# Expert rows fetched and turned one place at a time, 13 weight slots, and the smallest expert last

## What is computed

```python
def moe_ffn(h, comb, wg, wu, wd):
    out = jnp.zeros_like(h)
    for e in range(N_EXPERTS):
        ye = (jax.nn.silu(h @ wg[e]) * (h @ wu[e])) @ wd[e]
        out = out + comb[:, e:e + 1].astype(h.dtype) * ye
    return out

    h2 = (rms_norm(x, p['norm2_w']) * (1 + sc2) + sh2).reshape(bt * s, D_MODEL)
    comb = route(h2, w_router, router_bias)      # two weights a token, the rest zero
    y_moe = moe_ffn(h2, comb, ...).reshape(bt, s, D_MODEL)
    x = x + g2 * y_moe
    y = rms_norm(x, final_norm_w)
```

## Time and profile before

| | us |
|---|---|
| median of three runs (lowest, highest) | 1006.31 (1005.38, 1008.71) |
| the profiled execution: its own time | 1004.06 |
| its span, first to last instruction | 1002.3 |
| busy in the span: PE, DVE, ACT, POOL | 944.0, 441.4, 233.2, 145.3 |
| mean rate of the DMA engines over the span | 236 GB/s |
| mean granted PE clock (share of full speed) | 0.986 |

### The profile page before, as it was taken

How to read it: one execution, slowest core, us unless ns; L and a number is a source line. 1 busy time by engine, 2 the same in 40 slices (tenths; PEclk the granted TensorE clock), 3 DMA queues, 4 the chain that set the end, 5 groups by cost and what they waited for, 6 DMA issues and landing times.

```text
span 1002.3 us, 18836 instructions
## 1 busy us (share of the span) xinstructions
PE 944.0 (94%) x7702; PEld 659.7 (66%) x7702; DVE 441.4 (44%) x1094; ACT 233.2 (23%) x461; POOL 145.3 (14%) x236
## 2 busy tenths in 40 slices
PE   5999999999999999999999999999899988797895
PEld 2667666666666666666666777767599856564671
DVE  3221234676346986656641531134643342322316
ACT  2231222243263322232252300002231110110013
POOL 0000232343020343322300000011200000000010
PEclk9999999999999999999999999999999999899997
DMA  9943344564455655665443533342579999999973
GB/s 376 392 165 126 127 169 143 197 225 162 161 193 197 255 196 179 227 218 202 159 172 126 224 122 127 126 168 98 214 291 387 419 419 420 417 420 420 421 281 118
DMA packets 46541, 236.98 MB, mean 236 GB/s; under 512 B 6672, under 2 KB 10352, under 8 KB 23152
## 3 DMA queue, kind: packets, MB, share of 16 engines
q1 hardware_dynamic: 44480, 229.83, 59.7%
q0 software_dynamic: 1520, 5.34, 1.6%
q10 hardware_dynamic: 448, 0.50, 0.1%
HBM read 212.34 MB, written 23.31 MB: 235 GB/s over the span
## 4 chain that ended last, share of the span: by engine, by line
PE 73%; DMA 15%; DVE 6%; issue 2%; ACT 2%; SPq 1%; POOL 0%; POOLq 0%; DVEq 0%
PE pjB L884 15%; PE pjA L884 15%; DMA ring<-in_w 8%; PE pjA L1282 7%; PE pjB L1282 7%; DMA bp<-in_w 4%; PE states L1456 4%; PE states L1468 3%; PE states L1459 2%; DMA yd<-hF 2%; PE states L893 1%; PE bank L1019 1%; PE states L1261 1%; PE states L1019 1%; PE bank L1248 1%
## 5 line engine op out<-in xcount | busy, mean ns | idle before, releaser
L884 PE MATMUL pjA<-hF,ring 128*128 128x320 f32 x608 | 171.9, 436 | 0.5 <-ACT regA L1719 0.5
L884 PE MATMUL pjB<-hF,ring 128*128 128x320 f32 x608 | 171.8, 435 | 0.0
L884 PEld LDWEIGHTS pjA<-hF,ring 128*128 128x128 f32 x608 | 113.2, 190 | 50.7 <-issue 7.0
L884 PEld LDWEIGHTS pjB<-hF,ring 128*128 128x128 f32 x608 | 113.3, 190 | 48.6 <-issue 4.7
L1456 PE MATMUL states<-ring,oF 128*32 128x128 f32 x720 | 80.5, 273 | 2.1 <-DMA ring<-in_w 1.7
L1456 PEld LDWEIGHTS states<-ring,oF 128*32 128x32 f32 x720 | 78.0, 110 | 5.5 <-issue 2.7
L1459 PE MATMUL states<-ring,oF 128*32 128x384 f32 x720 | 80.7, 491 | 0.0
L2764 DVE TENSOR_TENSOR oF<-oF,states 128x256 f32<-128x256 f32 (+1 forms) x15 | 7.2, 483 | 139.9 <-PE states L1468 70.4
L2470 DVE TENSOR_TENSOR G<-G 128x320 f32<-128x320 f32 x32 | 47.1, 1510 | 0.0
L2076 POOL TENSOR_TENSOR G<-regA,G 128x128 f32<-128x128 f32 (+1 forms) x32 | 19.0, 594 | 192.3 <-ACT G L1775 192.3
L2173 POOL DMA_DIRECT2D yd<-hF x1 | 0.6, 640 | 244.2 <-DVE hF L2755 244.2
(11 more groups left out here) (565 smaller groups left out, 1518.2 us busy)
## 6 DMA issues: line engine op xcount, KB each, us to landing
ring<-in_w SPq DMA_DIRECT2D x144, 1024.0 KB, 8.5
rF<-in_w SPq DMA_DIRECT2D x11, 1024.0 KB, 18.6
bcF<-in_w SPq DMA_DIRECT2D x11, 1024.0 KB, 20.6
bp<-in_w SPq DMA_DIRECT2D x10, 1024.0 KB, 19.0
G<-in_ss SPq DMA_DIRECT2D x16, 512.0 KB, 4.7
out_ss_new<-G SPq DMA_DIRECT2D x16, 512.0 KB, 2.9
G<-csd SPq DMA_DIRECT2D x16, 320.0 KB, 3.5
G<-in_sg SPq DMA_DIRECT2D x4, 1024.0 KB, 6.4
```

What stands on the lines that cost most here:

```text
L884: mm = pe.matmul(pj[g % 2][:, 0:T], w[:, k, half * P:half * P + P], hF[:, k, :], start=(k == 0), stop=(k == KT - 1))
```

## The change

The places: `FULL_AT` becomes (0, 1, 4, 6, 8, 10), six instead of eight. Only places 0 and 1 are fixed; the smallest expert stands in place 15, with two blocks. The loop is written out, without a hardware loop.

The slots: 13 instead of 9. The new ones lie in `xsF` (two, loaded before the experts start) and in `regA` (two, loaded right behind the branch: the first when x has been turned, the second when the token rows are no longer needed).

The rows: `xd` is read place by place, 96 or 64 rows (`rows_in`, SP), turned by PE (`turn_rows`) and copied by ACT and DVE (`copy_rows`) into one of two buffers. The later turnings of weights and gates (`turn_late` 6 to 11) go behind the `gate_up` of places 6 to 11. A store of 96 rows of x behind `xd`'s end, early in the kernel, makes reading at full width defined.

The stores to `yd` are issued by ACT instead of SP.

The end: place 15's tokens are finished in a layout of their own, 64 rows as two halves of 512 values. PE collects in one bank, for these rows, what the other expert, the gate and x have given (`base_rows`, three tiles); DVE multiplies the last `down` with the weight and the gate (`weighted_half`), adds the bank, and scales. The three output tiles are written without these rows' last part, and then POOL writes the finished rows over them by an indirect DMA, which waits for all three. The additions of x for the first two tiles move from DVE to POOL.

```diff
-SLOTS = R + 3
+SLOTS = R + 7
+KNOWN = R + 5
-FULL_AT = (0, 1, 2, 5, 8, 11, 14, 15)
-FIXED_AT = (0, 1, E - 1)
+FULL_AT = (0, 1, 4, 6, 8, 10)
+FIXED_AT = (0, 1)
...
+            def rows_in(p):
+                at = sp.value_load(meta[0:1, ROW_AT + p:ROW_AT + p + 1], min_val=0, max_val=XROWS)
+                sp.wait_ge(s_xt2, max(p - 2, 0))
+                sp.dma_start(rowsB[p % 2][0:cap_of(p), :], d["xd"][bass.ds(at, cap_of(p)), :]).then_inc(s_xe[p % 2], 16)
...
             with sp.If(few(sp)):
+                sp.wait_ge(s_tm, 6)
+                sp.dma_start(slot(KNOWN), d["w"][chunk_row(*SEQ[KNOWN])]).then_inc(slot_ready(KNOWN)[0], 16)
                 sp.wait_ge(s_xd, 16 * 6)
-                sp.dma_start(xs01[:, 0, :], d["xd"][0:P, :]).then_inc(s_xe[0], 16)
-                sp.dma_start(xs01[:, 1, :], d["xd"][P:2 * P, :]).then_inc(s_xe[1], 16)
-                sp.wait_ge(s_oss, GH + 1)
-                sp.dma_start(hT, d["xd"][2 * P:XROWS, :].rearrange("(a p) c -> p a c", p=P)).then_inc(s_xe[1], 16)
...
+                rows_in(1)
+                sp.wait_ge(s_oss, GH + 2)
+                sp.dma_start(slot(KNOWN + 1), d["w"][weight_row(2) + SEQ[KNOWN + 1][1]]).then_inc(slot_ready(KNOWN + 1)[0], 16)
+                rows_in(2)
+                refill(0, 0, 4)
+                rows_in(3)
...
+                for p in range(3, LAST):
+                    refill(p, 0, 4)
+                    if p + 3 < E:
+                        rows_in(p + 3)
+                    refill(p - 1, 4, 6)
...
+                gate_up(0)
+                turn_rows(1)
+                gate_up(1)
+                turn_rows(2)
+                down(0)
+                turn_rows(3)
+                down(1)
+                gate_up(2)
+                for p in range(3, LAST):
+                    gate_up(p)
+                    turn_rows(p + 1)
+                    if TM_EARLY <= p < 12:
+                        turn_late(p)
+                    if p == 12:
+                        last_rows()
+                    down(p - 1)
+                down(LAST - 1)
+                gate_up(LAST)
+                turn_act()
+                base_rows(0)
+                down(LAST)
+                base_rows(1)
+                base_rows(2).then_inc(s_gw, 1)
+                row_sums()
...
+            def base_rows(t):
+                pe.wait_ge(s_base if t == 2 else s_x3, 1 if t == 2 else t + 1)
+                for h in range(2):
+                    mm = each_row(b[4], selL, hT[0:TT[t][2], t, 512 * h:512 * h + 512], t, h, t == 0, t == 2)
+                return mm
...
+                for t in range(2):
+                    pool.wait_ge(s_gm, t + 1)
+                    pool.tensor_tensor(hT[:, t, :], hT[:, t, :], xT[:, t, :], ALU.add).then_inc(s_x3, 1)
+                pool.wait_ge(s_tix, 2)
+                pool.wait_ge(s_f, 4)
+                pool.wait_ge(s_out, 16 * 4)
+                pool.indirect_dma_start(out=d["yrows"], out_offset=bass.IndirectOffsetOnAxis(ap=tix[:, 0:1], axis=0),
+                                        in_=zF_, in_offset=None).then_inc(s_last, 16)
...
+                summed(0).then_inc(s_gm, 1)
+                gated_up(LAST)
+                turned_last()
+                summed(1).then_inc(s_gm, 1)
+                cm(summed(2))
+                cm.wait()
+                dve.tensor_tensor(hT[0:NSAMP, 2, :], hT[0:NSAMP, 2, :], xT[0:NSAMP, 2, :], ALU.add).then_inc(s_base, 1)
+                final(0, 0, y2)
+                dve.wait_ge(s_gwc, 3)
+                weighted_half(0)
+                weighted_half(1)
+                final(1, 1, y2)
+                dve.wait_ge(s_zl, 2)
+                dve.wait_ge(s_gw, 2)
+                dve.tensor_tensor(zL, zL, b[4][:, :], ALU.add).then_inc(s_zl, 2)
+                final(2, 2, y2)
```

## The result

The changed kernel takes 1020.45 us (median of 4 runs, 1019.66 to 1023.96) against 1007.08 for the kernel before in the same job: ratio 1.014, 95% interval 1.011 to 1.017. It is slower by 1.4%. 997.4 had been forecast, a range of 987 to 1005.5, and a chance of 0.07 for slower. The profiled execution's span is 1018.3 us against 1002.3, and against 993.4 in the forecast.

A forecast was written before the change was run, and what follows sets the result against it. It took the weight stream's end and the tail behind it as the bounds: stream end 961, first gathered rows 965.9, plus 17.5 and 10.0 gives a span of 993.4 (1002.3 before), time 997.4, range 987 to 1005.5 us.

The forecast's parts named there:

- The stream: Weight stream after the branch: fewer bytes, earlier start and less idle time move its end from 971.0 to 961 us.
- rival 4: Row loads in SP's single queue starve the weight stream, DMA idling at every place: slower; 0.07 together with anything unforeseen.
- a DMA share under 0.95: Sign set beforehand: such a share between 750 and 940 us would show the forecast wrong.
- Start and idle time: Weight stream: loads into new slots start at 716.5, winning 0.9 us; closing the stall at 730 to 750 wins 6.1.
- Six large places for eight at nothing: Experts: fewer three-block places save PE 11.3 us, costed at nothing because loads hide them from place 5 on.
- The store of place 14: Stream's end: issued on ACT's queue at 948.9, it takes 7.8 us and lands at 956.7, 14.3 us earlier.
- the prediction's first reading: Engines take turns between queues with work, so place 14's store on ACT's queue overtakes the weight chunks, taking 7.8 us.
- the second: Issuing engines save only issue time, so place 14's store takes 16.1 us and the end comes 8.3 us later.
- rival 3: Place 14's store is no quicker on ACT's queue (16.1 us); tail shifts 8.3 us, time 1005.7, no change; chance 0.08.
- The tail: After the stores: first gathered rows at G = 965.9, PE's work until G + 17.5, then 10.0 us to 993.4.
- The end part: Behind PE's last base rows: DVE's addition and scaling, output, final scatter and waits, 10.0 us in all.
- One sign: Sign set beforehand: more than 31 us from the first gather issue to the end would show the forecast wrong.

The follow-up runs named there:

- e1_wide: Changed kernel, row loads bringing the same bytes as pieces of 2 or 3 KB into all 128 partitions (wrong rows): 995.67 us, ratio 0.988.
- e1_from_w: Changed kernel, row loads reading from the weights' tensor instead of xd, into the same partitions (wrong rows): 1023.99 us.
- e1_one_row: Changed kernel, row loads from place 3 on bringing one row, same issue point and wait (left-over rows used): 988.98 us.
- e1_halves: Changed kernel, result kept, rows loaded as halves (some as quarters) over all 128 partitions, PE turning 128x128 blocks: 995.24 us, ratio 0.988.
- e2_mid: Changed kernel, row loads from place 3 on written 32 partitions higher (32 to 95, or 32 to 127), same 4 KB pieces: 1004.28 us.
- e3_upper: Changed kernel, row loads from place 3 on written to the uppermost partitions (64 to 127, or 32 to 127): 1024.17 us.
- e3_pair: Changed kernel, each row load from place 3 on split into two DMAs, half to partitions from 0, half to partitions from 64: 1019.25 us.
- e2_rows128: Changed kernel, result kept, every row load bringing 128 rows into all partitions whatever the place's size: 1003.07 us, ratio 0.996.
- e2_sp_store: Kernel of e1_halves, stores to yd issued by SP behind the refills instead of by ACT: 1000.11 us, ratio 0.994.
- e2_eight: Kernel of e1_halves with eight places of three blocks instead of six: 996.6 us, ratio 0.990.
- e3_tail_dve: Kernel of e1_halves, the tail's two additions of the base rows on DVE instead of POOL: 994.17 us, ratio 0.987.

## Why the prediction was wrong, step by step

All kernels' numbers together, in us but for the rate (GB/s, 750 to 950; time: median, or the one run):

```
kernel        time     span     excess  rate
before        1007.08  1002.3    8.7    416
changed       1020.45  1018.3   32.1    377
e1_wide        995.67   995.1    7.5    420
e1_from_w     1023.99  1022.2   35.6    371
e1_one_row     988.98   987.0    8.9    420
e1_halves      995.24   993.1    7.1    420
e2_mid        1004.28  1002.2   15.8    407
e3_upper      1024.17  1022.2   33.7    372
e3_pair       1019.25  1017.5   29.0    382
e2_rows128    1003.07   998.1    6.7    420
e2_sp_store   1000.11   998.8    7.2    420
e2_eight       996.60   996.4    7.1    420
e3_tail_dve    994.17   992.3    7.0    420
```

The kernel before, measured beside each group of these runs, took 1006.96 to 1007.08, so the groups can be compared. From the first gather to the end of the span the changed kernel takes 34.8 us and its variants 34.0 to 35.4 (e1_one_row 36.8): nearly all that sets them apart lies ahead of the tail.

**The step that failed** is in "The stream": "the rows are read expert by expert at the places' full width ... (4.3 MB, 1.7 MB more)", at 416 GB/s. The row loads were priced by their bytes, and by a rate measured where every load fills all 128 partitions. The kernel before has no load into 64 or 96 partitions in its stream: its sorted rows come in whole, 128 partitions at a time, and its stores read from 64 or 96 without loss. A load into a part of the memory was thus an operation that this stretch of before does not show, and I gave it neither a price of its own nor a bound. It costs 1.7 us apiece beyond its bytes, 25.0 us in all; the forecast of 997.4 missed the 1020.45 by 23.1. The count in the same term is off as well: places 1 to 15 read 5 x 96 + 10 x 64 = 1120 rows, not 1056. The load that was left out has 0.3 MB, 0.6 us. That the idle time per place might exceed 1.0 us was written down as rival 4, but with another mechanism (SP's order), which e1_one_row and e1_halves exclude, and with a sign to look for, a DMA share under 0.95, that did not show: the share was 1.02.

**The rest came out close**, and e1_halves lets it be checked against numbers. Its span is 993.1, the forecast was 993.4. That they agree to 0.3 us is partly luck: in the tail the sum held and the mechanism did not.
- Start and idle time: the first load of the new slots goes out at 716.42 in the changed kernel (716.5 forecast), and the hole at 730 to 750 is closed.
- Six large places for eight at nothing: right. Undone, PE's busy time grows by 8.7 us and the time by 1.4.
- The store of place 14: gathers in e1_halves start at 958.04 (forecast near 957), in the changed kernel the store takes 7.1 us to land (7.8). That agrees with the prediction's first reading, by which it overtakes the chunks; the second, 16.1 us on ACT's queue too (rival 3), is excluded by this 7.1. What the queue is worth to the whole kernel is 4.9 us, not 8.3, and by way of place 12's store.
- The tail, in e1_halves from the first pair of rows G:

```profile
965.29 1.15 ACT L2047 ACTIVATE regA<-regA,G 128x1024 f32<-128x1024 f32 x1 [8.89 <-DMA xsF<-yd,idx]
...
969.10 2.34 POOL L2242 TENSOR_TENSOR regA<-regA,G 128x1024 f32<-128x1024 f32 x1 [3.93 <-DVE regA L2796]
...
979.60 1.08 PE L1517 MATMUL bank<-regA,G 64*64 64x512 f32 x4 [1.06 <-DVE regA L2910]
...
982.91 0.68 DVE L2918 TENSOR_TENSOR oF<-oF,bank 128x512 f32<-128x512 f32 x1
...
989.23 1.01 POOL L2246 DMA_INDIRECT out_y<-oF,tix  x1 [12.02 <-DMA out_y<-xsF]
```

G is 965.29 (965.9 forecast), POOL's addition ends at G + 6.15 (6.2), PE's last base rows at G + 15.4 (17.5). PE was forecast to be what the tail waits for, but that last product itself waited for DVE. PE was quicker than priced: it was idle for 9.70 us and ran at half clock behind that, as forecast, but only until 974.4, and the last two chunks took 2.40 and 1.90 us, not 3.6 and 2.8. The end part took 993.1 - 980.7 = 12.4, not 10.0: behind PE's last product DVE still has the weighting of place 15's two halves and the scaling of one row block ahead of the last addition (982.91). Two errors of 2 us with opposite signs cancel.
- One sign was set badly: more than 31 us from the first gather to the end was to mean wrong, but the forecast itself has 36 (957 to 993.4), and e1_halves has 35.1.

What the change set out to win is thus there: against before, e1_halves has its first gather 13.7 us earlier (958.04 for 971.78) and 4.5 us more behind it, 9.2 in the span.

Open: why a one-sided load of 0.6 us costs its neighbours 1.7. The packet records don't name the engine or the partition of a piece, so who waits for whom could not be read.

## What to carry to other kernels

Ask of each new load in a full DMA stream which partitions it writes, not only how many bytes it has. Here the loss was gone when the partitions below 64 and those from 64 on had equal shares within one DMA, and splitting rows into halves over all 128 partitions did that at no cost in PE time (PE is busy for 927.0 us of the span, 941.1 in the changed kernel). Read the rate beside the busy share: the share was 1.02 at 377 GB/s and 1.02 at 420. And where the trace of before has no row for an operation, the sum needs a bound for it even when its bytes are known.

## What the runs showed of the hardware that was not expected

- A DMA into 64 partitions on one side of partition 64, or into 96 with two thirds of them on one side, in a stream of weights, slowed the pieces of 8 KB that started while it passed from 309 ns to a mean of 375 to 527 (load by load in the changed kernel, for 4.5 to 9.6 us). Either side did so (excess 32.1 and 33.7 us); 32 to 95 did not (at most 0.2 us a load), 32 to 127 did (0.9 to 2.2 in e2_mid).
- Stores that read 32, 64 or 96 partitions did not: in e1_halves, with 30 of them, the rate is 420.
- A product of 64x1024 values on DVE and an addition of 128x1024 on POOL took 3.28 and 3.35 us side by side, 1.22 and some 2.2 alone.
